# Adding a norm's squares with one VectorE reduce at three places, and the high products of two weight chunks ahead of the low ones at two

## What is computed

```python
hn = rms_norm(h, attn_norm_g[l])
...
x = x + rmsnorm(mix, g_mix_post[i])
f = swiglu(rmsnorm(x, g_ffn_pre[i]), w_gate_up[i], w_down[i])
x = x + rmsnorm(f, g_ffn_post[i])
gate = jax.nn.sigmoid(rmsnorm(x, g_ple[i]) @ w_ple_gate[i])
x = x + gate * (p[i] @ w_ple_proj[i])
```

## Time and profile before

| | |
|---|---|
| median of 3 runs | 1896.39 us (1894.56 to 1898.91) |
| the profiled execution | 1895.68 us |
| its span in the trace | 1893.9 us |
| TensorE busy | 1846.5 us, 97% |
| VectorE, ScalarE, GpSimd busy | 914.5, 613.3 and 571.6 us |
| memory traffic | 87 GB/s over the span |

### The profile page before, as it was taken

How to read it: one execution, slowest core, us unless ns; L and a number is a source line. 1 busy time by engine, 2 the same in 40 slices (tenths; PEclk the granted TensorE clock), 3 DMA queues, 4 the chain that set the end, 5 groups by cost and what they waited for, 6 DMA issues and landing times.

```text
span 1893.9 us, 22795 instructions
## 1 busy us (share of the span) xinstructions
PE 1846.5 (97%) x8690; PEld 1504.4 (79%) x8694; DVE 914.5 (48%) x1129; ACT 613.3 (32%) x886; POOL 571.6 (30%) x365
## 2 busy tenths in 40 slices
PE   8999999999999999999999999999998999999988
PEld 6897788888888876788888888777785888888866
DVE  6745763333335765543333335597546332333364
ACT  4236722122223335422212224234435222322342
POOL 3310355141325430252324155221115210211252
PEclk9999999999999999999999999999998999999998
DMA  4434332232222234225232222311121222222221
GB/s 173 142 111 96 96 112 89 89 111 89 98 102 89 89 114 117 91 93 141 89 104 96 89 98 98 121 67 45 45 101 61 95 92 104 93 102 99 89 88 67
DMA packets 40558, 183.94 MB, mean 97 GB/s; under 512 B 5512, under 2 KB 12200, under 8 KB 21416
## 3 DMA queue, kind: packets, MB, share of 16 engines
q1 hardware_dynamic: 38224, 179.26, 28.0%
q10 hardware_dynamic: 2264, 3.72, 1.0%
HBM read 161.99 MB, written 3.67 MB: 87 GB/s over the span
## 4 chain that ended last, share of the span: by engine, by line
PE 86%; DVE 8%; ACT 2%; POOL 2%; issue 1%; DMA 1%; SPq 0%; DVEq 0%; ACTq 0%; POOLq 0%
PE ps L495 23%; PE ps L496 23%; PE ps L497 23%; PE ps L545 3%; PE ps L534 3%; PE ps L535 3%; PE ps L672 1%; DVE xb L1422 1%; PE ps L863 1%; PE ps L881 1%; PE ps L786 1%; PE ps L776 1%; DVE wlo L1416 1%; DVE probs L1546 1%; PE ps L579 1%
## 5 line engine op out<-in xcount | busy, mean ns | idle before, releaser
L1416 DVE TENSOR_TENSOR wlo<-raw,whi 128x2048 fp32r<-128x2048 f32 x142 | 352.1, 2480 | 324.4 <-ACT whi L972 324.0
L972 ACT ACTIVATE whi<-raw 128x2048 fp32r<-128x2048 f32 x149 | 284.3, 1908 | 382.6 <-PE ps L497 272.6
L495 PE MATMUL ps<-xb,whi 128*128 128x512 f32 x1024 | 402.8, 393 | 2.8 <-DVE wlo L1416 1.6
L497 PE MATMUL ps<-xb,wlo 128*128 128x512 f32 x1024 | 400.0, 391 | 0.0
L496 PE MATMUL ps<-xb,whi 128*128 128x512 f32 x1024 | 399.9, 391 | 0.0
L495 PE MATMUL ps<-xa_hi,whi 128*128 128x512 f32 x788 | 308.7, 392 | 3.2 <-DVE wlo L1416 3.2
L497 PE MATMUL ps<-xa_hi,wlo 128*128 128x512 f32 x788 | 307.8, 391 | 0.0
L496 PE MATMUL ps<-xa_lo,whi 128*128 128x512 f32 x788 | 307.7, 390 | 0.0
L495 PEld LDWEIGHTS ps<-xb,whi 128*128 128x128 f32 x1024 | 193.3, 189 | 45.9 <-issue 3.3
L497 PEld LDWEIGHTS ps<-xb,wlo 128*128 128x128 f32 x1024 | 193.1, 189 | 40.8
L496 PEld LDWEIGHTS ps<-xb,whi 128*128 128x128 f32 x1024 | 193.4, 189 | 39.8 <-issue 0.2
(11 more groups left out here) (311 smaller groups left out, 2516.9 us busy)
## 6 DMA issues: line engine op xcount, KB each, us to landing
raw<-wst SPq DMA_DIRECT2D x149, 1024.0 KB, 4.8
stage<-qk_split SPq DMA_DIRECT2D x64, 128.0 KB, 2.4
h<-xT ACTq DMA_DIRECT2D x4, 512.0 KB, 8.0
stage_k_lo<-qk_split SPq DMA_DIRECT2D x32, 64.0 KB, 2.0
mla_qn<-q_nope SPq DMA_DIRECT2D x8, 256.0 KB, 2.7
mla_v<-v_tok SPq DMA_DIRECT2D x8, 256.0 KB, 2.7
outT<-h SPq DMA_DIRECT2D x8, 256.0 KB, 2.0
bias_scratch<-bias_rows ACTq DMA_DIRECT2D x1, 1536.0 KB
```

The source lines that it names most:

```text
L495: pe.matmul(out, lhs_hi, rhs_hi, start=first, stop=False)
L497: return pe.matmul(out, lhs_lo, rhs_hi, start=False, stop=last)
L972: act.activation(whi[slot][:, :], raw[slot][:, :], ACT.Copy).then_inc(whi_done, 1)
L1416: dve.tensor_tensor(wlo[slot][:, :], raw[slot][:, :], whi[slot][:, :].bitcast(F32), ALU.subtract).then_inc(wlo_done, 1)
```

## The change

The sums of squares of norms 0 (first norm), 9 (ahead of gate/up) and 11 (ahead of ple) move from seven GpSimd adds to one VectorE `tensor_reduce` over k. At gate/up and at ple, a new function on TensorE, `features_two`, takes two chunks together: the products with high activations of both, then those with low activations of both, with the statistics between the low products of the first and of the second, and the broadcast ahead of the last k. ScalarE makes the second chunk's high part after its sixth part and all squares after the eighth; VectorE makes the second chunk's low part after its first low half. `linear` for ple is written out, with its last two chunks outside a loop.

```diff
--- before.py
+++ after.py
@@ -73,7 +73,7 @@
 
 
 SQUARED = (8, 8, 8, 2, 3, 8, 16, 0, 8, 8, 8, 8)
-ADDED = (7, 7, 7, 1, 2, 7, 14, 0, 7, 7, 7, 7)
+ADDED = (1, 7, 7, 1, 2, 7, 14, 0, 7, 1, 7, 1)
 N_NORMS = len(SQUARED)
 SQ = [sum(SQUARED[:n]) for n in range(N_NORMS + 1)]
 SSQ = [sum(ADDED[:n]) for n in range(N_NORMS + 1)]
@@ -546,6 +546,35 @@
                             if k == kt - 1:
                                 mm.then_inc(tile_done, 1)
 
+            def features_two(c, t0, xhi, xlo, fresh, norm):
+
+
+                parts = [[w[(c + j) % 2][:, :].rearrange("p (k m) -> p k m", k=KD) for w in (whi, wlo)] for j in range(2)]
+                for j, (w_hi, w_lo) in enumerate(parts):
+                    pe.wait_ge(wlo_done, c + j + 1)
+                    for a in range(2):
+                        bank_ready(t0 + 2 * j + a)
+                    for k in range(KD):
+                        if j == 0:
+                            pe.wait_ge(fresh[0], fresh[2] + k + 1)
+                        for a in range(2):
+                            out, m = ps[(t0 + 2 * j + a) % 4][:, :], slice(a * P, (a + 1) * P)
+                            pe.matmul(out, w_hi[:, k, m], xhi[:, k, :], start=(k == 0), stop=False)
+                            pe.matmul(out, w_lo[:, k, m], xhi[:, k, :], start=False, stop=False)
+                for j, (w_hi, _) in enumerate(parts):
+                    if j == 1:
+                        stat(norm)
+                    for k in range(KD):
+                        if j == 0:
+                            pe.wait_ge(fresh[1], fresh[2] + k + 1)
+                        elif k == KD - 1:
+                            broadcast(norm)
+                        for a in range(2):
+                            out, m = ps[(t0 + 2 * j + a) % 4][:, :], slice(a * P, (a + 1) * P)
+                            mm = pe.matmul(out, w_hi[:, k, m], xlo[:, k, :], start=False, stop=(k == KD - 1))
+                            if k == KD - 1:
+                                mm.then_inc(tile_done, 1)
+
             def tokens(slot, c, t0, xhi, xlo, per=0, i=0):
 
                 pe.wait_ge(wlo_done, c + 1)
@@ -938,8 +967,7 @@
             def gate_up(r, n, first):
                 c, t = C[f"gu{r}"], T[f"gu{r}"]
                 if first:
-                    features(c % 2, c, t, xb_hi, xb_lo, fresh=(xh_done, xl_done, X["ffn"]))
-                    features((c + 1) % 2, c + 1, t + 2, xb_hi, xb_lo, hook=lambda k: late_rstd(9, k))
+                    features_two(c, t, xb_hi, xb_lo, (xh_done, xl_done, X["ffn"]), 9)
                 with pe.Fori(1 if first else 0, n // 2) as i:
                     for s in range(2):
                         features((c + s) % 2, c + s + 2 * i, t + 2 * s, xb_hi, xb_lo, per=4, i=i)
@@ -958,7 +986,10 @@
             proj(1, None)
 
 
-            linear("ple", 2, xb_hi, xb_lo, (xh_done, xl_done, X["ple"]), norm=11)
+            c, t = C["ple"], T["ple"]
+            features_two(c, t, xb_hi, xb_lo, (xh_done, xl_done, X["ple"]), 11)
+            for s in range(2):
+                features((c + s) % 2, c + 2 + s, t + 4 + 2 * s, xb_hi, xb_lo)
 
 
         @block.scalar
@@ -1348,11 +1379,9 @@
                 squared = 0
                 for k in range(KD):
                     part(k)
-                    if k in (0, 2, 5):
-                        square(squared)
-                        squared += 1
-                hi(C[stage] + 1, 0, T[stage])
-                for k in range(squared, KD):
+                    if k == 5:
+                        hi(C[stage] + 1, 0, T[stage])
+                for k in range(KD):
                     square(k)
 
             proj(0)
@@ -1422,6 +1451,11 @@
                 dve.scalar_tensor_tensor(out=dst, in0=src, scalar=scale, in1=dst_hi.bitcast(F32),
                                          op0=ALU.mult, op1=ALU.subtract).then_inc(xl_done, 1)
 
+            def sum_squares(squares, n):
+
+                dve.wait_ge(sq_done, SQ[n] + KD)
+                dve.tensor_reduce(ssq[:, :], squares[:, :, :].rearrange("p k n -> p n k"), AX.X, ALU.add).then_inc(ssq_done, 1)
+
             def mean_square(n, dim):
                 dve.wait_ge(stat_done, STATS[n] + 1)
                 dve.tensor_scalar(ms_t[:, 4 * n:4 * n + 4], STAT[:, 0:QT], 1.0 / dim, EPS, ALU.mult, ALU.add).then_inc(ms_done, 1)
@@ -1444,6 +1478,7 @@
             for k in range(KD):
                 x_lo(xa_lo[:, k, :], h[:, k, :], g("attn0", k), xa_hi[:, k, :], X["qkv"] + k)
             lo(1, 1)
+            sum_squares(squares0, 0)
             dve.wait_ge(const_loaded, 16 * len(consts))
 
             for j in range(2):
@@ -1959,6 +1994,8 @@
                     elif k == 5:
                         add(4)
                 for k in range(KD):
+                    if k == 1:
+                        lo(c_next + 1, (c_next + 1) % 2)
                     x_lo(xb_lo[:, k, :], h[:, k, :], g(gnext, k), xb_hi[:, k, :], x0 + k)
 
             dve.wait_ge(x2_done, 1)
@@ -1971,11 +2008,12 @@
                 def pair(i):
                     for s in range(2):
                         j = HID2 + 8 * r + 2 * i + s
-                        if not (first and isinstance(i, int) and s == 1):
+                        if not (first and isinstance(i, int)):
                             lo(c + s + 1 + 2 * i, (c + s + 1) % 2)
                         if first and isinstance(i, int) and s == 0:
+                            sum_squares(squares2, 9)
+                            mean_square(9, D)
                             lo(c + 2, c % 2)
-                            mean_square(9, D)
                             take_rstd(9)
                         tt = t + 2 * s
                         tile_ready(tt, 4, i)
@@ -2018,9 +2056,9 @@
                 dve.wait_ge(gated_done, k + 1)
                 dve.tensor_tensor(h[:, k, :], h[:, k, :], projected[:, k, :], ALU.add).then_inc(y_done, 1)
 
-            for j in (1, 2):
-                lo(c + j, (c + j) % 2)
+            sum_squares(squares2, 11)
             mean_square(11, D)
+            lo(c + 2, c % 2)
             take_rstd(11)
             for u in range(4):
                 for a in range(2):
@@ -2070,7 +2108,7 @@
                 rstd(n)
 
             pool.wait_ge(dve_const, 1)
-            add_squares(squares0, 0)
+            rstd(0)
 
 
             def rope(t, dst1, dst2, rope_tmp, per=0, i=0):
@@ -2195,7 +2233,7 @@
                 for k in RES_POOL:
                     pool.wait_ge(branch_done, KD * n0 + k + 1)
                     pool.tensor_tensor(h[:, k, :], h[:, k, :], branch[:, k, :], ALU.add).then_inc(res_pool, 1)
-                add_squares(squares2, n)
+                rstd(n)
 
             add_squares(squares2, 8)
             onto_residual(0, 9)
```

## The result

The changed kernel takes **1878.26 us** (median of 4 runs, 1877.86 to 1878.72) against 1897.02 for the kernel before on the same chip (1894.56 to 1898.91): a ratio of 0.9905, 95% interval 0.9893 to 0.9916. The profiled execution took 1877.93 us with a span of 1876.1, so 17.8 us of span are gone. The direction and the places were as forecast and the time lies in the range, but 24.3 us were forecast. Where the time went is read from the same views as before.

What follows compares the result with a forecast made beforehand. TensorE, busy 97%, was taken as the bound, with its idle and half-speed time to win. 8.7 + 8.6 + 8.6 = 25.9, less 1.6 for the clock, gave 24.3 and 1872 us; range 1868 to 1880.

Steps and rivals of the forecast that it cites:

- What bounds: TensorE busy 97%; its waits come from VectorE's low halves, slow beside GpSimd's adds, at start, gate/up and ple.
- low halves stay slow: Rival: GpSimd is not the cause; gate/up and ple gain 2.6 each, the start 4; 1887 us, chance 0.07.
- The price of the reduce: VectorE's stepped reduce over 4096 elements at each norm: 4.4 us at 1.036 ns per element, upper end 10.4.
- The middle bound of 7 us: Reduce at 1.6 times the contiguous price, from chunk 1's low part at the start taking 3.36 us, priced at 2.1.
- The slow-reduce rival: Stepped reduce takes 6.5 to 9 us; start loses the excess, other places what exceeds cover; 1876 to 1882, chance 0.33.
- Start: First norm: low halves at 0.74 each, broadcast at 27.3 instead of 34.53, chunk 2 at 33.8; gain 8.7 us.
- Gate/up and ple: Last two places: both chunks' high products run together, low halves speed up, the reduce is hidden; gain 8.6 us each.
- The reduce hidden with 1.5 us to spare: At gate/up the reduce ends at 1462.1, before TensorE's low products of chunk one end at 1463.6.
- The new idle of 1.7: TensorE waits 1.7 us before chunk three while VectorE's norm copy, gate and up empty both banks behind the broadcast.
- The clock: The new idle pieces may bring half-rate products costing 0 to 1.6 us at each place; 1.6 deducted in all.
- Slower: Rival: the reduce alone makes the kernel slower, needing 15 us of reduce; 1906 at 17 us, chance 0.03.
- not doing what it says: Case that GpSimd's adds remain at the three norms; ruled out because the statistics' wait count falls from 7 to 1.

Runs made afterwards that it cites:

- the three adds: Changed kernel with the stepped reduce replaced at all three norms by three contiguous VectorE adds of halves: 1872.04 us, ratio 0.9872.
- the second profile: Profile of the unchanged changed kernel, run again as the base for the experiments: 1876.75 us, ratio 0.9893.
- the copy of one tile: Changed kernel with the reduce replaced by copying the first of eight square tiles, a wrong norm made only as a bound: 1873.33 us, ratio 0.9877.
- the last experiment: Kernel with three contiguous adds and broadcast ahead of k = 5, ScalarE making chunk two's high part after part 2 instead of 5: 1867.6 us, against 1868.53 without.

## Why the prediction was right, and where it was off

**What bounds.** Right. The low halves were the bound at both places, and GpSimd's adds made them slow: 1760 to 747 ns in the median, and 12.57 to 5.38 us in the old order with the adds replaced. What the prediction didn't ask is how much of the 8.6 us each half of the change brings: the new order alone brings all of what the two bring together. The rival "low halves stay slow" (1887) is out.

**The price of the reduce.** This step failed. 4.4 us were taken "because the contiguous reduces are the same operation". All three times it took this (line 1457 of the changed kernel, ns at least, median, at most):

```profile
L1457 DVE TENSOR_REDUCE ssq<-squares x3: 7299/7469/7471, 20.1 to 1831.7; 128x512 f32<-128x4096 f32 x3
```

7.4 us for 4096 elements are 1.81 ns each, against 1.08 when read contiguously. The middle bound of 7 us was the near one, by luck: it came from a subtraction that ran beside GpSimd's adds (3.36 us in the earlier trace rows, 2.29 without them), and a neighbour's slowdown says nothing of a step. The rule of the Trainium skill (Vector Engine (DVE) Microarchitecture Reference, section "Measured stream behaviour on trn2") is borne out: it gives 1.73 ns per column for a source that hops at every element, and this reduce, whose step is 2 KB, took 1.78 to 1.82. It applies to a one-source reduce too, which I had left open.

**The slow-reduce rival** is what happened, and its law comes out near. At 7.3 us the excess r is 2.9; the start loses r, the others r - 2 each: 2.9 + 0.9 + 0.9 = 4.7, so 1872 + 4.7 = 1876.7. (The prediction takes 2 us of cover here and 1.7 in its own sums; with 1.7 it is 5.3.) The changed kernel measured 1878.26 at first and 1876.75 when run again; the three adds, which take the excess away, gave back 4.7 in the medians. That the figures meet to 0.1 is luck. The law keeps the 1.6 deducted for the clock, which wasn't needed, and at gate/up and ple it gives 7.7 where 6.6 was gained; between the two profiled executions the adds gave back 4.4 + 1.4 + 1.3 = 7.1.

**Start, 8.7 forecast, 4.7 measured.** All up to the reduce's start was right within 0.1 us. Behind it 2.9 were lost to the reduce, and the second profile shows just that: chunk 2 began at 36.68, 2.9 later than forecast. In the first profile TensorE's half speed took more: statistics 1.87 long instead of 1.05, broadcast 1.91 instead of 1.13, and the six products between them 0.43 apart instead of 0.23, so chunk 2 began at 39.22. The rest of the way evened this out to 0.5 us. The power stayed at 1.02 us as assumed, but not for the reason given. In the first profile VectorE's low part did run beside it (29.74 to 32.03, the power 29.66 to 30.68); the power was short because it started 0.08 us earlier. With the copy of one tile it started second and took 2.92.

**Gate/up and ple, 8.6 forecast, 6.6 measured, at each.** Chunk two directly behind chunk one: right. The reduce hidden with 1.5 us to spare: wrong. It took 3.1 us more, so 1.6 of wait would have been due; it started 0.6 us sooner than forecast and TensorE came 0.3 later, which left 0.73. The statistics came 22.0 us after the first high product instead of 20.9, the broadcast 26.5 instead of 24.9 (statistics and fourteen products together 4.4 for 4.0, and 0.15 of wait for the power, taken at 1.02 but 3.15 long). The power's collision with VectorE's next low part was foreseen as a risk for the start and overlooked here; the fourteen products hid all but 0.15. The wait for part 6, put at 0.4, was 1.10, yet the high products of both chunks ended only 0.15 us later than forecast (17.47 us after the first of them, 17.32 forecast). The new idle of 1.7 was right to 0.03, and its cause too: moving the broadcast earlier halved it. With the three adds the distance from first high product to chunk three is 1461.60 - 1433.12 = 28.48, a gain of 8.0.

**The clock, 1.6 deducted.** Not needed: the granted clock is 1.00 from 1459 to 1468, and also behind the new idle of 1.73 us, from 1467.8 to 1480 and from 1847 to 1858. The half speed came at the start, behind the wait of 2.80, where I had put none. The two errors partly cancel.

**Slower, and not doing what it says.** Neither: the adds are gone from GpSimd, and the reduce stayed at half of the 15 us that the slower case needed.

What stays open: why TensorE's clock falls behind the wait of 2.8 us in four profiles and not in the fifth, and whether the order of the last experiment is worth its 0.6 us. Not tried: starting the power ahead of VectorE's low part at the two norms whose branch is added to h just ahead of gate/up and ple, where it takes 2.99 and 3.00 us in the kernel before and TensorE waits 1.9 and 1.8 for it.

## What to carry to other kernels

Price a reduce by the step with which it reads, and not by its element count alone: here, with the reduced axis the outer one, adding halves with contiguous two-input operations was the cheaper way. Before two remedies for one wait are added up, ask what each leaves for the other: here the order alone carried the gain at gate/up and ple, and the reduce mattered only where nothing covered it. When a long operation becomes short, look at which two operations then meet and which of them starts first, and at where the last result must be ready before the next tiles.

## What the runs showed of the hardware

- A VectorE reduce over 128 x 4096 fp32 takes 7.27 to 7.47 us when it reads with a step of 2 KB (all kernels that have it), 4.42 us when it reads neighbours. Three contiguous adds of the same data take 4.26 us from start to end.
- ScalarE pays for a step too: in a row of four, a square of 128 x 512 written 32 bytes apart takes 1.04 us, contiguous 0.54.
- GpSimd's power on 128 x 4 elements takes 1.02 us alone. When VectorE's 128 x 2048 subtraction (2.29 us) has started 0.02 to 0.23 us ahead of it, it takes 2.92 to 3.15 and ends 0.87 to 0.89 after the subtraction. When the power starts first, by as little as 0.08 us, it keeps its 1.02 and the subtraction its 2.29 (changed kernel at the start; GpSimd's adds in the new order at gate/up, 0.31 us ahead).
- VectorE's low halves take 0.74 us alone and 1.78 beside GpSimd's adds, in either order of the work.
- The same wait of 2.80 us at the start was followed by 7 us at a granted clock of 0.51 in one profile of the changed kernel, and by full speed in the other. Of the eight profiles with a wait of 1.8 to 2.8 us ahead of the statistics or the broadcast at the start, seven show the 1.2 GHz level behind it; the four without such a wait (three adds) stay at a granted clock of 1.00 from 24 to 38 us. Waits of 1.73 us at gate/up and ple were followed by full speed.
